# Latents stage of a trunk layer: the first block's key tile is loaded and normalised ahead of its query tiles, two value projections of cached tokens run ahead, and the second block's sums run later

## The reference, cut to what matters

```
def rmsnorm(x, g):
    y = x * lax.rsqrt(jnp.mean(x * x, axis=-1, keepdims=True) + EPS)
    return y * g
...
    proj = h @ p['w_in']
    conv_in, q_a, kv_a, k_rope, gate_lin = jnp.split(proj, IN_SPLITS, axis=-1)
    q = (rmsnorm(q_a, p['q_norm']) @ p['w_qb']).reshape(B, n, N_HEADS, QK_NOPE + QK_ROPE)
    ckv = rmsnorm(kv_a, p['kv_norm'])
    keys_ckv = jnp.concatenate([ctx_ckv, ckv], axis=1)
    kv = (ckv @ w_kvb).reshape(B, S, N_HEADS, QK_NOPE + V_DIM)
    k_nope, v = kv[..., :QK_NOPE], kv[..., QK_NOPE:]
```

## Time and profile before

| | us |
|---|---|
| median of 3 runs | 3183.33 (3180.16 to 3183.79) |
| the profiled execution | 3184.42 |
| its span, first to last instruction | 3182.6 |
| TensorE busy | 2928.4 |
| VectorE busy | 1934.8 |
| ScalarE busy | 1084.9 |
| GpSimd busy | 1061.3 |

### The profile page before, as it was taken

The page is one execution under the profiler, slowest core; times in us unless marked ns, Lnnn a source line. Parts: engine busy times, 40 slices in busy tenths (PEclk is TensorE's granted clock), DMA queues, the critical chain, the costliest instruction groups (busy, mean ns, idle before and its releaser), DMA issues. The chain is left out here.

```text
span 3182.6 us, 43970 instructions
## 1 busy us (share of the span) xinstructions
PE 2928.4 (92%) x16924; PEld 2348.9 (74%) x16924; DVE 1934.8 (61%) x2561; ACT 1084.9 (34%) x1718; POOL 1061.3 (33%) x686
## 2 busy tenths in 40 slices
PE   6999999999789999999999979979954999999993
PEld 2888888888667777777777757768834888888882
DVE  4418393839347777777777746545674555555565
ACT  4411111111344444444444423213422344343434
POOL 0000000000123343444333535421214766666652
PEclk8999999999889999999999999989976999999996
DMA  5312222211540101110110136574414566666667
GB/s 210 109 54 105 76 105 80 105 64 67 177 140 10 27 19 26 25 33 13 27 25 6 60 94 205 173 242 163 158 54 141 184 199 204 202 212 200 207 187 281
DMA packets 139524, 371.26 MB, mean 117 GB/s; under 512 B 20886, under 2 KB 47996, under 8 KB 129116
## 3 DMA queue, kind: packets, MB, share of 16 engines
q1 hardware_dynamic: 99820, 266.47, 25.3%
q0 software_dynamic: 23984, 74.71, 8.3%
q10 hardware_dynamic: 15552, 27.79, 2.5%
HBM read 265.99 MB, written 102.89 MB: 116 GB/s over the span
## 5 line engine op out<-in xcount | busy, mean ns | idle before, releaser
L1160 ACT ACTIVATE at_w<-at_sc 128x512 f32<-128x512 f32 (+1 forms) x592 | 346.3, 591 | 417.8 <-PE at_sc L1235 362.8
L1322 DVE TENSOR_REDUCE at_mpart<-at_mx 128x2 f32<-128x512 f32 x575 | 368.5, 683 | 167.0 <-PE at_mx L1262 166.9
L1210 POOL TENSOR_TENSOR at_part<-at_part,at_w 128x512 f32<-128x512 f32 x224 | 297.4, 1328 | 359.4 <-ACT at_w L1160 356.1
L2479 POOL TENSOR_TENSOR moe_gu_lo<-moe_raw_gu,moe_gu_hi 128x2048 fp32r<-128x2048 f32 x64 | 296.6, 4635 | 121.7 <-ACT moe_gu_hi L2545 121.3
L520 DVE SCALAR_TENSOR_TENSOR fr_r<-fr_r,fr_dw 128x2334 f32<-128x2334 f32 x120 | 318.0, 2650 | 3.9
L377 PE MATMUL fr_po<-hT_hi,fr_w_hi 128*128 128x512 f32 (+1 forms) x800 | 297.1, 371 | 3.1 <-PE fr_po L377 1.9
L377 PE MATMUL fr_po<-hT_hi,fr_w_lo 128*128 128x512 f32 (+1 forms) x800 | 294.7, 368 | 0.0
L377 PE MATMUL fr_po<-hT_lo,fr_w_hi 128*128 128x512 f32 (+1 forms) x800 | 294.6, 368 | 0.0
L1274 PE MATMUL at_acc<-at_w,V 128*64 128x256 f32 (+1 forms) x2368 | 289.7, 384 | 0.0
L2664 DVE TENSOR_TENSOR moe_d_lo<-moe_raw_d,moe_d_hi 128x1024 fp32r<-128x1024 f32 x64 | 184.1, 2876 | 105.3 <-ACT moe_d_hi L2576 105.3
L1349 DVE TENSOR_TENSOR at_part<-at_part,at_w 128x512 f32<-128x512 f32 x224 | 228.9, 1022 | 19.7 <-ACT at_w L1160 6.7
(11 more groups left out here) (391 smaller groups left out, 6800.5 us busy)
## 6 DMA issues: line engine op xcount, KB each, us to landing
moe_raw_gu<-w_gate_up SPq DMA_DIRECT2D x64, 1024.0 KB, 4.8
moe_raw_d<-w_down SPq DMA_DIRECT2D x64, 512.0 KB, 5.2
fr_wm<-w_ada_rows POOLq DMA_DIRECT2D x32, 512.0 KB, 4.1
gates_scratch<-fr_r ACTq DMA_DIRECT2D x64, 256.0 KB, 2.0
mx_gates<-gates_scratch SPq DMA_DIRECT2D x64, 256.0 KB, 3.1
fr_raw<-w_in SPq DMA_DIRECT2D x28, 512.0 KB, 5.1
fr_r<-x POOLq DMA_DIRECT2D x18, 512.0 KB, 4.6
raw<-mixed_scratch SPq DMA_DIRECT2D x9, 1024.0 KB, 6.2
```

Of the source, the lines that this page charges most:

```text
L1160: act.activation(w[:, g % NW, k, 0:n], sc[:, (2 * g + k) % SCB, 0:n], ACT.Exp, scale=SM_SCALE).then_inc(exp_done, 1)
L1210: pool.tensor_tensor(part[:, j % 2, 1, 0:n], before, w[:, g % NW, 1, 0:n], ALU.add).then_inc(add_p, 1)
L1322: dve.tensor_reduce(mpart[:, s, 2 * half:2 * half + 2, c], max_bank(m, half), AX.X, ALU.max).then_inc(red_done, 1)
L2479: pool.tensor_tensor(gu_lo[:, slot], raw_gu[:, slot], gu_hi[:, slot].bitcast(F32), ALU.subtract).then_inc(glo_done, 1)
```

## The change

In `load(0)` the block's one transfer becomes two, with the loads of the cached tokens and of `w_v` between them; a new semaphore `first_ld` tells of the key tile. Squares, sums, roots and scales get a second argument, `part`: in block 0 the key tile (part 0) and the query tiles (part 1) go separately, in the other blocks all three together as before. `high` becomes `high_kv` and `high_q`, `spread` takes a list of kinds, `norms` a list of tiles. On each engine the calls for blocks 0 and 1 are put in another order. POOL's instructions and their order are not edited.

```diff
-                sp.dma_start(cached[:], t["cache_ckv"]).then_inc(cached_ld, 16)
-                sp.dma_start(wv[:], t["w_v"]).then_inc(wv_ld, 16)
...
+                    if b == 0:
+                        sp.dma_start(lat[:, 0, 2, :], t["misc"][2 * P:3 * P, 0:BLK]).then_inc(first_ld, 16)
+                        sp.dma_start(cached[:], t["cache_ckv"]).then_inc(cached_ld, 16)
+                        sp.dma_start(wv[:], t["w_v"]).then_inc(wv_ld, 16)
+                        sp.dma_start(lat[:, 0, 0:2, :], t["misc"][0:2 * P, 0:BLK].rearrange("(k p) n -> p k n", p=P)
+                                     ).then_inc(lat_ld[0], 16)
+                        return
...
+    FIRST = (2, 3), (0, 2)
+
+    def stats(b):
+
+        return [(0, FIRST[0]), (1, FIRST[1])] if b == 0 else [(b + 1, (0, 3))]
...
-                squares(0)
+                squares(0, 0)
                 act.wait_ge(cached_ld, 16)
                 act.activation(ckv_hi[:, 0:PAST], cached[:], ACT.Copy).then_inc(cached_hi, 1)
-                roots(0)
                 act.wait_ge(wv_ld, 16)
                 act.activation(wv_hi[:], wv[:], ACT.Copy).then_inc(wv_split, 1)
+                roots(0, 0)
+                squares(0, 1)
+                roots(0, 1)
+                high_kv(0)
                 act.wait_ge(wk_ld, 16)
                 act.activation(wk_hi[:], wk[:], ACT.Copy).then_inc(wk_split, 1)
-                squares(1)
-                high(0)
+                squares(1, 0)
+                high_q(0)
...
-                sums(0)
-                spread(0)
-                sums(1)
+                sums(0, 0)
                 pe.wait_ge(cached_lo, 1)
+                pe.wait_ge(wv_done, 1)
+                project((0, "v", 0))
+                project((0, "v", 1))
+                sums(0, 1)
+                spread(0, (1,))
                 for b in range(NBL):
                     pe.wait_ge(clo_done, b + 1)
                     for o in OUT:
-                        if o[0] != b:
+                        if o[0] != b or b == 0 and o[1:] in (("v", 0), ("v", 1)):
                             continue
-                        if b == 0 and o[1:] == ("v", 0):
-                            pe.wait_ge(wv_done, 1)
+                        if b == 0 and o[1:] == ("k", 0):
+                            spread(0, (0,))
+                            sums(1, 0)
                         if b == 0 and o[1:] == ("k", 0):
                             pe.wait_ge(wk_done, 1)
-                        if o[1:] == ("k", 0) and b + 1 < NBL:
-                            spread(b + 1)
+                        if o[1:] == ("k", 2 if b == 0 else 0) and b + 1 < NBL:
+                            spread(b + 1, (1, 0))
...
-                scales(0)
+                scales(0, 0)
                 dve.wait_ge(gain_ld, 16)
-                norms(0)
+                norms(0, ((2, 1),))
+                scales(0, 1)
+                norms(0, ((0, 0), (1, 0)))
                 low(0)
```

More of the change, by code:

```diff
@@ L692, in _, with squares, roots, high_kv @@
             def _(act):
[L693 to L702 removed]
+                def squares(b, part):
+                    n, (k0, k1) = BLOCKS[b][1], stats(b)[part][1]
+                    if (b, part) == (0, 0):
+                        act.wait_ge(first_ld, 16)
+                    else:
+                        act.wait_ge(lat_ld[b % RING], 16 * (b // RING) + 16)
+                    if b:
+                        act.wait_ge(csum_done, b + 1)
+                    act.activation(sq[:, k0:k1, 0:n], lat[:, b % RING, k0:k1, 0:n], ACT.Square).then_inc(sq_done, 1)
+                def roots(b, part):
+                    at, (part, (k0, k1)) = 4 * b, stats(b)[part]
+                    act.wait_ge(csum_done, part + 1)
+                    for kind, size in ((0, QL),) * (k0 == 0) + ((1, KVL),) * (k1 == 3):
                         act.activation(root[:, b, kind, 0:TILES[b]], csum[:, at:at + TILES[b], kind, 0], ACT.Sqrt,
                                        scale=1.0 / size, bias=eps[:]).then_inc(root_done, 1)
[L706 removed]
+                def high_kv(b):
                     tok, n = BLOCKS[b]
@@ L824, in _ @@
                             if b + 2 < NBL:
[L825 removed]
+                                sums(b + 2, 0)
                         project(o)
@@ L857, in _, with scales @@
             def _(dve):
-                def scales(b):
-                    dve.wait_ge(root_done, 2 * b + 2)
-                    dve.reciprocal(rstd[:, b, :, 0:TILES[b]], root[:, b, :, 0:TILES[b]]).then_inc(rstd_done, 1)
-                    dve.wait_ge(rstd_done, b + 1)
+                def scales(b, part):
+                    number, (k0, k1) = stats(b)[part]
+                    kinds = (1, 0)[part if b == 0 else 0:1 if (b, part) == (0, 0) else 2]
+                    rows = slice(min(kinds), max(kinds) + 1)
+                    dve.wait_ge(root_done, number + 1 if b == 0 else 2 * b + 2)
+                    dve.reciprocal(rstd[:, b, rows, 0:TILES[b]], root[:, b, rows, 0:TILES[b]]).then_inc(rstd_done, 1)
+                    dve.wait_ge(rstd_done, number + 1)
                     wait(dve, bc_done, 2 * b)
-                    for kind in (1, 0):
+                    for kind in kinds:
                         for i in range(TILES[b]):
@@ L866, in scales, with norms @@
                                               ).then_inc(diag_done, 1)
-                def norms(b):
+                def norms(b, which):
                     n = BLOCKS[b][1]
-                    for k, kind in ((2, 1), (0, 0), (1, 0)):
+                    for k, kind in which:
                         dve.wait_ge(bc_done, 2 * b + 2 - kind)
```

46 lines of the change are left out of this document (19 added, 27 removed).

## The result

The changed kernel is slower: 3191.89 us (median of 9 runs, 3187.14 to 3196.16) against 3183.33 us for the kernel before in the same comparison (9 runs, 3173.51 to 3187.48). The ratio is 1.0031, 95% interval 1.0019 to 1.0043. A second comparison gave 3193.16 against 3186.20, ratio 1.0023 [1.0013, 1.0032]. The forecast was 3185.8 with a range to 3191.0. The profiled execution took 3195.96 us with a span of 3194.1.

The account below looks back on a forecast made before the run. The chain through block 2's load was taken to bound the latents stage's start. Its issue moved from 826.03 to 828.5 with the rest unchanged: +2.5 us on the path, 3185.8 against the median 3183.33, range 3180.8 to 3191.0.

Parts of the forecast that it names:

- the sum: Steps from value projections 0 and 1 to block 2's load issue: 826.1 at 2.4 GHz, 828.5 with the clock forecast.
- the stated bounds: Landing of block 0's key tile: at most 4.6 or 4.3 us, at least 2.0 or so; 3.3 taken.
- the 2.05 us of the earlier trace: Extra time of block 0's eight diagonals beside GpSimd's split (3.71 against 1.66 us), claimed to leave the path.
- The low-clock sum: Steps to block 2's load issue with TensorE at 1.2 GHz all the way: 4.5 us more, 830.6.
- The row that I carried over: Projection burst from 856.49 before the change: clock 0.50 until 859.85, 1.00 from 859.9.
- the other row: Sums alone before the change: clock 0.50 for the 5 us from 809.50, not raised by them.
- rival 2: Clock stays at 1.2 GHz until block 2's load is issued: +4.5 us, 3187.8; chance 0.20.
- the rest of the 10.8 us unchanged: From block 2's load issue to the first query projection: 10.8 us before, claimed the same after.
- Rival 3: Clock also still low when key projection 2 starts: +8.2 us, 3191.5, 0.26% slower; chance 0.11.
- Rival 1: Clock is up from the first value projections on and stays: 0.0 us, 3183.3; chance 0.14.
- Rival 4: TensorE's queue, not block 2's load, holds the query projections, so the lead is kept: 2.4 us earlier, 3180.9; chance 0.09.
- the cover: Wait for block 2's load, claimed to hide block 1's moved sums, which would otherwise cost 2.6 us (5.2 at 1.2 GHz).

Follow-up runs that it names:

- the later squares: Changed kernel with query sums and key spread first, GpSimd's splits exchanged, and squares and sums of block b+2 later: 3177.05 us, ratio 0.9972 [0.9963, 0.9981] against the kernel before.

## Why the prediction missed

**What held.** The place was right, and the chain was. Block 2's load was issued in the order of steps that the sum lists, and each fixed term came out near its size: value output 0 at 6.8 us into the stage (6.6 forecast), 824.55 - 819.88 = 4.7 us from the key spread's end to value output 2 (5.0), 832.41 - 828.59 = 3.8 from the query spread to the load (3.8). The key tile landed within 2.6 us, below the 3.3 taken. It is inside the stated bounds, but the lower one was worked out wrongly: 768 KB at 414 GB/s are 1.9 us, and 4.6 less 1.9 is 2.7, not 2.0, so the landing came just under the bound that those rows give. GpSimd's split of `wk` stood directly ahead of the key latents' split. The eight diagonals in two groups of four took 0.87 us each at 812.20 and 820.87, so the 2.05 us of the earlier trace rows did leave the path, and by themselves brought nothing, as the sum had it. Here the trace agrees with SBUF — State Buffer, Who interferes with whom, of the Trainium skill, as far as it goes: GpSimd ran beside neither group.

**The step that failed is the clock in the sum.** The low-clock sum gave 830.6 - 803.2 = 27.4 us into the stage, and the load was issued at 27.4. That close a fit is partly luck: the key spread took 2.05 us (1.7 in the sum), the way to value output 2 took 4.7 (5.0) and the query spread 1.31 (1.7), and the misses cancel. I chose 25.3, because "A burst that begins at 809.8 would by that row be at full clock about 813.2". It was not: the window of 8.1 us from the first value output to the end of the key spread shows 0.50 throughout. The query sums took 3.41 us, the high price of the two (1.8 or 3.5), and the key spread 2.05. The row that I carried over, in the earlier trace rows, was of a burst that went on as projections. Here the projections lasted 2.7 us and sums of two columns followed, and the other row had already shown that 5.00 us of sums alone ran at 0.50. The nearer pair of rows pointed to rival 2.

**The second step that failed is "the rest of the 10.8 us unchanged".** It took 11.9. The squares of block 2 came 0.4 us sooner behind the load, but from key projection 2 to the first query output it took 844.34 - 838.67 = 5.7 us against 836.81 - 832.72 = 4.1, at a clock of 0.50 until 839.7 and 0.78 behind it. Three windows of TensorE alone (length, busy us, granted clock, DMA share, GB/s), first the same way in the kernel before, which ran at the full clock:

```profile
833.16:837.16 4.00, 4.00 (x32) 1.00 0.34 131
```

And the changed kernel, where the clock was up and had fallen before key projection 2:

```profile
827.05:831.05 4.00, 4.00 (x29) 0.90 0.06 18
831.05:835.05 4.00, 2.89 (x8) 0.53 0.34 91
```

The forecast let the shift reach "the end of the stage whole, apart from the clock", and never priced the clock: in this pair of profiles 1.6 us more up to block 3's load. From there to the end the two stages take 76.6 us each. The kernel before, executed again, took 2.7 us longer for this piece than the first time, so the 1.6 us are not shown to be the change's.

**Which rival it was.** Rival 3: the granted clock at key projection 2 was 0.50, the point from which it decides. Its price was +8.2 (4.5 + 1.2 + 2.5), measured were +7.2 (4.5 + 1.1 + 1.6); the 2.5 for block 2's sums was wrong, they took 2.73 us at the full clock, and the loss fell on the query projections instead. It gave 3191.5 and the median was 3191.9, but that fit is partly luck: 4.3 of the 11.5 us between the two spans lie outside the stage, and between the second executions of both kernels the stage differs by 2.7 us while the comparison has 7.0 between the medians. I gave it 0.11 and drew the range's upper end just below it. The low clock at key projection 2 was not simply rival 2 continued: the clock had risen to 0.90 and fell again while TensorE was busy for 2.89 of 4.00 us, and it did the same in the second execution (0.88, then 0.55, then 0.50). Rival 1 fell: the work that the change pulled forward ran at 0.50 and left the clock there. By TensorE: Matmul & The Clock Gate, Part 1, of the Trainium skill, activity releases the clock; the trace agrees only in part, since 8.02 busy us of 8.10 did not release it, and the added products did so for the second half. Rival 4 fell: the wait for a bank was there again (0.67 us at 838.66), and taking block 2's squares out of its way brought the first query output 2.6 us sooner.

**The moved sums** "cost nothing" as long as the cover was there, and it was. Alone they cost 2.9 us at the first query output. The 2.6 that the prediction names for that case is near it by chance: it is their time in TensorE's queue, and the run shows the cost on another way, ScalarE's idle 4.07 us ahead of block 2's squares.

**What the prediction didn't see** is that nothing of the change required the query spread to stand behind value outputs 2 and 3. The sum contained it (1.4 or 2.6 of projections ahead of it), and the prediction took the sum's result and not its cause: moving this one call gives the kernel before its time back.

## What to carry to other kernels

Before work is pulled forward in an in-order queue, follow the chain that frees the buffer of the next load, and keep that chain's steps ahead of work whose result nobody waits for; here one call in the wrong place cost 4.5 us at the load and some 5.5 at the first query output, and an order without that wait, which also had the clock up for the query spread, won 0.28% (0.19 to 0.37) with the later squares. Behind a start-up phase full of waits, price TensorE's work at the lower clock unless a row shows the higher one for the same kind of work in the same sequence, and carry that price on to the work behind it. Rank kernels whose medians lie within 5 us by moments in the trace that repeat, and only then by their times.

## What the runs showed of the hardware

- The granted clock stayed at 0.50 through 8.1 us in which TensorE was busy 8.02 us: six value products of 512 columns, 16 passes of sums of 2 columns that kept it busy for 3.41 us, and two spread passes. With twenty added products of 128 columns whose result nobody reads it was 0.95 from 826.10 on. The median was then 2 to 3 us lower (3189.74 against 3191.89 and 3193.16), which is not clear of noise: the intervals of the ratios overlap.
- The same kernel before ran its stage in 123.4 and in 128.1 us, with the same order and starts equal to 0.3 us up to the first query output. In the longer one the clock was at 0.50 for 8 us from 866.25 on. What decides between the two was not found.
- The start of the stage, in front of which nothing was edited, lay between 803.16 and 809.87 us over the profiled executions. Single executions of the kernel before ranged from 3173.51 to 3194.78 us.
